# Mixture-of-experts stage of a hybrid backbone: 128-row items in split fp32r replaced by 64-row steps in plain fp32, in two column groups

## The reference

```python
def moe(h, w_router, b_router, w_gate, w_up, w_down):
    s = jax.nn.sigmoid((t @ w_router).astype(F32))
    sel = s + b_router.astype(F32)
    ...
    out = jnp.zeros_like(t)
    for e in range(N_EXPERTS):
        y = (jax.nn.silu(t @ w_gate[e]) * (t @ w_up[e])) @ w_down[e]
        out = out + combine[:, e:e + 1] * y
    return out.reshape(shp)
```

## Time and profile before

| | |
|---|---|
| median of 3 runs | 1831.44 us (1830.01 to 1834.89) |
| the profiled execution's own time | 1832.41 us |
| its span | 1830.6 us |
| PE / PEld / DVE / ACT / POOL busy | 1616.0 / 1274.2 / 1271.1 / 1096.7 / 38.9 us |
| mean granted TensorE clock | 0.954 |
| bytes by DMA | 376.58 MB, mean 206 GB/s |
| expert pieces loaded | 420 of 512 KB (35 items x 12) |
| layer 0, units up to the router | 0 to 530 us |
| layer 0, router and experts | 530 to 1034 us |
| layer 1, units | 1066 to 1418 us |
| layer 1, router and experts | 1418 to 1809 us |

### The profile page before, as it was taken

One profiled execution on the slowest core, in us unless ns is written; L12 is line 12 of the kernel. 1 busy time (PEld: TensorE's weight loads), 2 busy tenths in 40 slices (PEclk: granted clock), 3 DMA queues, 4 the chain that ended last, 5 costly groups with the idle time before them and its releaser, 6 DMA issues.

```text
span 1830.6 us, 24613 instructions
## 1 busy us (share of the span) xinstructions
PE 1616.0 (88%) x7922; PEld 1274.2 (70%) x7922; DVE 1271.1 (69%) x1685; ACT 1096.7 (60%) x1330; POOL 38.9 (2%) x38
## 2 busy tenths in 40 slices
PE   6799999999985999999999468889999599999994
PEld 4677776777753777777777356788788377777773
DVE  5847656654626777777777377588765688888884
ACT  5833354433424777778778257536544588888882
POOL 0000000000300000000000100000002000000000
PEclk9989999999997999999999787999999799999997
DMA  9753311213111777777777565553342378888883
GB/s 349 260 229 115 116 69 47 88 51 115 48 69 68 276 298 298 298 298 298 298 298 298 207 230 211 184 184 116 115 159 73 130 305 320 318 320 318 319 319 115
DMA packets 88961, 376.58 MB, mean 206 GB/s; under 512 B 10208, under 2 KB 12452, under 8 KB 74692
## 3 DMA queue, kind: packets, MB, share of 16 engines
q1 hardware_dynamic: 83482, 360.94, 52.4%
q0 software_dynamic: 2368, 10.62, 1.6%
q10 hardware_dynamic: 3050, 4.20, 0.6%
HBM read 347.41 MB, written 28.31 MB: 205 GB/s over the span
## 4 chain that ended last, share of the span: by engine, by line
PE 50%; issue 28%; DVE 9%; ACT 8%; DMA 3%; POOL 1%; ACTq 0%; DVEq 0%; POOLq 0%; SPq 0%
PE bank L1366 7%; PE bank L1367 7%; PE bank L1368 7%; PE bank L1638 4%; ACT whi L511 3%; DVE wlo L822 2%; PE bank L1694 2%; PE bank L1665 2%; PE bank L1664 2%; PE bank L1666 2%; PE bank L1696 2%; PE bank L1695 2%; PE bank L1344 2%; PE bank L1398 2%; PE bank L1399 1%
## 5 line engine op out<-in xcount | busy, mean ns | idle before, releaser
L822 DVE TENSOR_TENSOR wlo<-stage,whi 128x1024 fp32r<-128x1024 f32 (+1 forms) x314 | 496.5, 1586 | 76.0 <-ACT whi L511 71.0
L511 ACT ACTIVATE whi<-stage 128x1024 fp32r<-128x1024 f32 (+1 forms) x314 | 419.5, 1341 | 165.4 <-PE bank L1696 72.5
L1366 PE MATMUL bank<-h_hi,whi 128*128 128x512 f32 (+1 forms) x640 | 225.0, 352 | 9.9 <-DVE h_lo L822 7.8
L1664 PE MATMUL bank<-whi,xg_hi 128*128 128x512 f32 x560 | 227.1, 406 | 0.0
L1665 PE MATMUL bank<-wlo,xg_hi 128*128 128x512 f32 x560 | 221.2, 395 | 0.0
L1666 PE MATMUL bank<-whi,xg_lo 128*128 128x512 f32 x560 | 221.2, 395 | 0.0
L1367 PE MATMUL bank<-h_lo,whi 128*128 128x512 f32 (+1 forms) x640 | 220.1, 344 | 0.0
L1368 PE MATMUL bank<-h_hi,wlo 128*128 128x512 f32 (+1 forms) x640 | 219.8, 343 | 0.0
L822 DVE TENSOR_TENSOR wlo<-stage_b,whi 128x1024 fp32r<-128x1024 f32 x140 | 165.1, 1221 | 67.5 <-ACT whi L511 67.5
L511 ACT ACT_TABLE_LOAD x113 | 145.0, 1283 | 8.3 <-issue 6.3
L511 ACT ACTIVATE whi<-stage_b 128x1024 fp32r<-128x1024 f32 x140 | 141.2, 1060 | 9.8 <-PE bank L1666 9.8
(11 more groups left out here) (263 smaller groups left out, 2664.4 us busy)
## 6 DMA issues: line engine op xcount, KB each, us to landing
stage<-in_expert SPq DMA_DIRECT2D x210, 512.0 KB, 7.5
stage_b<-in_expert SPq DMA_DIRECT2D x140, 512.0 KB, 9.3
stage<-in_mod SPq DMA_DIRECT2D x48, 1024.0 KB, 5.0
stage<-in_in SPq DMA_DIRECT2D x40, 1024.0 KB, 4.8
stage_c<-in_expert SPq DMA_DIRECT2D x70, 512.0 KB, 5.0
y_rows<-yrow SPq DMA_DIRECT2D x37, 512.0 KB, 3.0
stage<-in_out SPq DMA_DIRECT2D x8, 1024.0 KB, 4.8
x_spill<-xT SPq DMA_DIRECT2D x2, 2048.0 KB, 11.7
```

The lines of the kernel that those rows point to most:

```text
L511: return nc.scalar.activation(out_, in_, f, **kw)
L822: return V.tensor_tensor(o, x, y, op)
L1366: MM(o, w[0], x_[0], start=start, stop=False)
L1664: MM(o, xg_hi[:, kk, :], hi[:, k, :], start=(kk == 0), stop=False)
```

## The change

The experts' weights are no longer split: `expert` is laid out as 4 pieces of 1 MB with gate and up side by side and 2 pieces for down, and `wexp` holds two experts (slots 0 and 1), over the old `stage`, `whi`, `wlo`, R1 and part of R2. Matmuls take plain fp32 operands. A step has C = 64 rows; the tokens `xg` (128x64) or the products `act_a` are the stationary operand, and the two halves of a piece (h = 0, 1) go to output partitions 0 to 63 and 64 to 127 of the same bank.

Experts are ranked by load on the device. A fixed plan (`CAPS`, `ORDER`) gives each rank a number of steps and the sequence of steps: 27 in layer 0 and 18 in layer 1, written out without a loop; `ExpertPlan` puts the ranks on the slots so that each expert is loaded once. What exceeds the caps goes to extra steps in a `Fori` of `count` turns, which reload the expert into slot 1; rank 15 has no step in the plan, so `count` is at least 1. With the counts above it is 1 in both layers. In layer 0 SP waits for slot 0's last use before it loads the extra expert, since the next layer's first units go to the same place.

Token rows are no longer gathered by matmuls. POOL scatters each 128-token block twice by indirect DMA into `x_rows` in HBM, at `rowid`; ACT waits for all of it and loads 64 rows per step (256 KB) on its own DMA queue. The output is written by ACT's queue as two DMAs of 128 KB per step. `x_rows` and `y_rows` (2816 rows each) are zeroed in layer 0 by 44 DMAs of 512 KB from HBM to HBM on SP, two behind each of 22 units from ("in", 1) on.

```diff
+C = 64
+CAPS = ((4, 4, 4, 2, 2, 2) + (1,) * 9, (2, 2, 2) + (1,) * 12)
+ORDER = ((1, 1, 1, 1, 13, 5, 5, 2, 9, 12, 2, 4, 4, 10, 2, 8, 2, 6, 0, 0, 7, 11, 0, 14, 0, 3, 3),
+         (6, 0, 0, 11, 7, 2, 2, 5, 13, 3, 1, 1, 4, 8, 10, 12, 9, 14))
...
+        wexp = at_byte("wexp", [P, 2, EC, 2048], f32, R1 - 72 * 1024)
...
-                        for b in range(NE + 1, NI + 1):
-                            load("all", "y_zeroed", y_rows[b * P:(b + 1) * P, :], zero_rows[:, :])
+                    if l == 0 and at["in", 1] <= n < at["in", 1] + ROWS // P:
+                        b = n - at["in", 1]
+                        load("all", "rows_zeroed", x_rows[b * P:(b + 1) * P, :], A["c_zero"])
+                        load("all", "rows_zeroed", y_rows[b * P:(b + 1) * P, :], A["c_zero"])
...
+                sp.wait_ge(S("lo"), NU)
+                sp.wait_ge(S("zr"), total)
+                sp.wait_ge(S("ranked"), 1)
+                for r in plan.loads:
+                    e = sp.value_load(rank_i[0:1, r:r + 1], min_val=0, max_val=NE - 1)
+                    for j in range(EC):
+                        if plan.before[r] > 0:
+                            sp.wait_ge(S(f"used{plan.slot[r]}{j}"), plan.before[r])
+                        expert_unit(e, plan.slot[r], j)
+                if l < DEPTH - 1:
+                    for n in range(RING):
+                        sp.wait_ge(S(f"used0{n}"), plan.uses[0])
...
+                with sp.Fori(0, count) as i:
...
+                        sp.wait_ge(S(f"used1{j}"), i + plan.uses[1])
+                        expert_unit(e, 1, j)
...
+                pool.wait_ge(S("rowid_ok"), 1)
...
+                        pool.indirect_dma_start(
+                            out=x_rows, out_offset=bass.IndirectOffsetOnAxis(ap=rowid[:, 2 * t + c:2 * t + c + 1], axis=0),
+                            in_=trow[:, t, :], in_offset=None,
+                        ).then_inc(S("scattered"), 16)
...
+                act.wait_ge(S("scattered"), 2 * NT * 16)
+                for s, (z, use, fill, row) in enumerate(plan.steps):
+                    if s > 0:
+                        act.wait_ge(S("xT_mm"), s)
+                    load_rows(slice(row, row + C))
+                    if s > 1:
...
+                        y_out(s - 2, slice(row_, row_ + C))
+                    if s > 0:
...
+                        silu(s - 1)
...
+                def gate_up(s, z, fill):
+                    pe.wait_ge(S("xg"), s + 1)
+                    for j in range(4):
+                        pe.wait_ge(S(f"ew{z}{j}"), fill * 16)
+                        for k in range(2):
+                            kk = 2 * j + k
+                            for h in range(2):
+                                c = slice((2 * k + h) * 512, (2 * k + h + 1) * 512)
+                                ins = MM(bank[0][h * C:(h + 1) * C, :], xg[:, kk, :], wexp[:, z, j, c], start=(kk == 0), stop=(kk == KT - 1))
+                        ins.then_inc(S(f"used{z}{j}"), 1)
...
+                for s, (z, use, fill, row) in enumerate(plan.steps):
+                    gate_up(s, z, fill)
+                    if s + 1 < STEPS:
+                        columns(s + 1)
+                    if s > 0:
+                        down(s - 1, *(plan.steps[s - 1][i] for i in (0, 2)))
+                    turn(s)
```

More of the change, by code:

```diff
@@ new lines, in _ @@
+                end = ends[:, 0, 8:]
+                v.then(tt(starts, end, chunks, SUB))
+                v.then(ts(move, starts, float(C), float(plan.extra_base), MUL, ADD))
+                v.then(tt(move, move, cap, SUB))
+                v.then(tt(move, move, base_, SUB))
+                pos = e3(bank[7][:, 0:W])
+                each = lambda x: x.unsqueeze(1).to_broadcast([P, NT, NE])
+                v.step(tt(e3(row(6)), pos, each(cap), ALU.is_ge))
+                v.then(tt(e3(row(7)), pos, each(base_), ADD))
@@ new lines, in _ @@
+                v.then(tt(e3(row(6)), e3(row(6)), each(move), MUL))
+                v.then(tt(row(7), row(7), row(6), ADD))
+                for c in range(2):
+                    v.then(tt(row(6), row(7), row(3 + c), MUL))
+                    v.then(V.reduce_sum(tokv[:, 4 + c, 0:NT], e3(row(6)), AX.X))
+                    ins = V.tensor_copy(rowid[:, c:c + 2 * NT - 1:2], tokv[:, 4 + c, 0:NT])
+                    if c == 0:
+                        v.then(ins)
+                    else:
+                        ins.then_inc(S("rowid_ok"), 1)
@@ new lines, in _ @@
+                columns(0)
+                for s, (z, use, fill, row_) in enumerate(plan.steps):
+                    dve.wait_ge(S(f"used{z}3"), use)
+                    pairs()
+                    if s + 1 < STEPS:
+                        columns(s + 1)
+                    product(s)
+                count = dve.value_load(count_i[0:1, 0:1], min_val=1, max_val=plan.extra)
+                with dve.Fori(0, count) as i:
+                    columns(i + STEPS)
+                    dve.wait_ge(S("used13"), i + plan.uses[1] + 1)
+                    pairs()
+                    product(i + STEPS)
@@ L1699, in _, with columns @@
-                pick_rows(0, 0, 4 * NT)
-                pick_columns(0, 0)
-                pick_columns(0, 1)
-                pick_rows(1, 0, 4 * NT)
-                with pe.Fori(0, last) as i:
-                    item(i, True)
-                item(last, False)
+                pe.wait_ge(S("row_a"), NT)
+                pe.wait_ge(S("row_d"), NT)
+                plan = plans[l]
+                STEPS = len(plan.steps)
+                def columns(s):
+                    pe.wait_ge(S("xload"), (s + 1) * 16)
+                    if not isinstance(s, int):
+                        pe.sem_inc(sem("all", "passed"), 1)
+                    for k in range(KT):
+                        ins = T_(bank[1][:, k * C:(k + 1) * C], xpick[:, k * P:(k + 1) * P], C)
+                    ins.then_inc(S("xT_mm"), 1)
@@ new lines, in _ @@
+                down(STEPS - 1, *(plan.steps[STEPS - 1][i] for i in (0, 2)))
+                pe.wait_ge(S("items_ok"), 1)
+                count = pe.value_load(count_i[0:1, 0:1], min_val=1, max_val=plan.extra)
+                with pe.Fori(0, count) as i:
+                    s = i + STEPS
+                    columns(s)
+                    gate_up(s, 1, i + plan.loaded[1] + 1)
+                    pe.wait_ge(S("act_a"), s)
+                    turn(s)
+                    down(s, 1, i + plan.loaded[1] + 1)
```

486 lines of the change are left out of this document (201 added, 285 removed).

## The result

The changed kernel takes 1855.17 us (median of 4 runs, 1854.11 to 1857.29), the kernel before 1830.72 (4 runs, 1826.51 to 1834.89): ratio 1.0135, 95% interval 1.011 to 1.0161. It is slower by 1.35%, where 1687 us were forecast. The profiled execution took 1857.29 us, its span 1855.1.

The account below looks back on a forecast made before the run. It took PE's matmuls to bound the expert stages, with splits on DVE and ACT and the DMA engines close behind. 1832.4 - 74 (layer 0) - 69 (layer 1) - 2 (gather) = 1687 us; range 1655 to 1805.

Parts of the forecast that it names:

- The rows' load: Expert steps: the next step's 64 rows land in 3.0 us, under 5.3 us of cover, so the load costs nothing.
- rows late: Rival, chance 0.11: row loads beside a full weight queue take 7.3 us, baring 2.0 us per layer 0 cycle, 54 us: 1741 us.
- The scatters: Start of layer 0's expert stage: last scatter lands 7.2 us behind its issue, at 591; first gate matmul at 598.
- The extra step: End of each layer's expert stage: one unplanned step that overlaps nothing and takes 25 us.
- PE's cycle: Each planned expert step: 10.3 us of fully overlapped matmuls, 1.7 of transposes, 0.5 of switching, 12.5 us in all.
- an estimate of 13.0 us: Rival, chance 0.06: two column groups give only 1.6 times, matmuls of a step 13.0 us, cycle 15.2: 1798 us.
- Layer 1 held by the DMA engines at 407 GB/s: Layer 1's expert stage: 112.8 MB take 277 us, so it ends at 1740 instead of PE's 1719, a gain of 69.
- The zero fill: SP's unit loads: zeroing grows from 7 to 44 DMAs of 512 KB and costs 0 us (0 to 10).
- The units unchanged: Before the expert stage: the units before 530 us keep their times.

Follow-up runs that it names:

- the order run: Against the changed kernel with three xpick buffers: all products of column group 0 first, then all of group 1, instead of alternating; 1981.64 us (one run).

## Why the prediction was wrong, step by step

- **The rows' load, "costs nothing at 3.0 us"**: this step failed. The flight was taken from writes that SP issues on its own queue; in the trace of the kernel before, no expert piece was in flight when any of the 37 was issued. Measured with two or more weight loads in flight it is 6.0 to 11.6 us, 10.5 at the median, against a cover of 5.3 forecast and 5.7 found (723.8 less 718.1). It was bare in 26 of 43 steps, 118 us, and 23 in the extra steps; the clock behind the pauses took 51 more (the 41 and 10 of the sum above).
- **The rival "rows late"** named the mechanism and missed the size. It took 7.3 us of flight from the earlier trace rows, so 2.0 a cycle, in layer 0 alone. Measured are 56 us in 13 steps of layer 0 and 62 in 13 of layer 1, 4.3 and 4.8 each. In layer 1 I held a bare wait to be hidden by cycles of 17 us set by the weights; but 11.8 + 5.5 + 1.9 of slower down is 19 to 20 (columns at 1650.61, 1669.70 and 1689.87), which is more than 17. And no term priced the clock: in the earlier trace rows it stands at 1.00 because nothing paused.
- **ACT's own queue** had no term at all: the two writes of the step before stand right in front of the load. It cost 102 us in all, and how that divides is bounded above.
- **The scatters, "last lands some 7.2 us behind"**: up to 26.5. The prediction had SP's loads start at 568.6 and the scatters go out from 574 to 585, and didn't put the two together; its 7.2 us were read from gathers beside which two weight loads at most were in flight. First gate product 609.4, not 598; 20 us over both layers.
- **The extra step, 25 us**: 35 (last planned down ends at 1016.8, gather at 1051.6). Its load waits on ACT for the copy-out of yrow, which waits for the write before it; PE stood for 13.7 us where 5.5 were put: 4.6 until the load was issued (1016.8 to 1021.3) and 9.0 of flight, three times the 3.0 taken. The run without weight traffic has 15.2 here, and it too loads this expert. The rest of the ten is the lower clock behind the pause (gate and up in 9.0 us). With the load issued ahead the step takes 20.6 (954.9 to 975.5).
- **PE's cycle, 12.5 us**: right, 11.8. 10.3 for the products was 10.74 (7.09 + 3.65), 1.92 times faster than 20.6, and the order run shows that it is the groups. By the Trainium skill's 2.38 times for three groups (TensorE: Matmul & The Clock Gate, Part 3), taken as 1.6 for two, an estimate of 13.0 us stood against it; no run here has three groups.
- **Layer 1 held by the DMA engines at 407 GB/s**: not in the changed kernel (298 GB/s above), but right once the rows are on time: 408 at a share of 1.02 in the window shown, and 27.8 us of waits for wexp. The 19.9 us of such waits in layer 0 had no term. The Trainium skill (DMA: Bandwidth & Descriptors, Specifications) puts a core's limit at about 358 GB/s, half of what two cores share. This kernel runs on one core, and the window shown and the earlier trace rows are above it.
- **The zero fill, 0**: right, by the doubled fill. **The units unchanged**: 7.3 us early in this trace; the place of two buffers explains a few of them.

With the rows' load and the scatters mended the kernel takes 1703 us, and 1695 with ACT's queue freed. The forecast of 1687 is 8 to 16 us under them, but not by every term. Cycles are 0.7 us shorter than forecast, 30 us over 45 steps, and the extra step with its load ahead takes 21 us instead of 25; against that stand 60 to 66 us of waits for wexp, where the forecast had 21 us for layer 1 (1740 against 1719) and nothing for layer 0. The 1684 us of the run without weight traffic are near the forecast partly by luck: that run is free of these waits, and still has the long starts (48.9 and 37.8 us of waits) and extra steps.

Still open: how the 4 to 7 us that a full weight queue adds to a 256 KB load divide between its engines' queues and the memory was not tried.

## What to carry to other kernels

A small load takes its time from what is in flight when it is issued, so read its price from rows beside the traffic that the change will make, not beside that of the kernel as it is; and where the cover is within 3 us of the landing, issue it earlier. A step earlier took one more buffer here, and two steps earlier gained 133 us. Look at what stands ahead of it too, in its own queue and in the program of the engine that issues it. And where a burst of megabytes and a chain of small dependent transfers start together, let the small ones go first: holding back 12.6 MB of weights for 21 us (562.3 to 583.4) gained 17 us in layer 0, and the same in layer 1 another 3.

## What the runs showed that was not expected

- The landing of one kind of load, 256 KB from DRAM, median: 3.5 us with no weight traffic, 7.5 beside it, 8.2 beside it with 256 KB ahead in the same queue (in layer 1 8.0 and 10.4); indirect scatters 3.9 alone and 15.5 (26.5 at most) behind weights.
- A pause of 4 to 6 us on PE costs 1.2 to 2.7 us more in the products behind it: down takes 4.81 to 6.33 us against 3.65, at a mean granted clock of 0.70 in the one window read.
- Two products of 64 stationary columns in different column groups run nearly wholly beside each other in plain fp32, if they alternate: 32 records in 7.09 us, where 0.43 each would be 13.8. One group behind the other overlaps by some 1.5 us at the border.
- Moving two 16 KiB buffers in SBUF makes the fp32r products of 512 columns some 5 ns (1.3%) shorter each, and those of 256 columns some 4 ns longer.
